# Opening of a three-layer kernel: half-size condition loads, context rows moved behind the first turned products, filler matmuls, context squares added on GpSimd

## The reference, cut to what matters

```python
sh1, sc1, g1, sh2, sc2, g2 = ada_mod(c, ada_w[0], ada_b[0])        # silu(c) @ w + b, w is 1024 x 6144
csh1, csc1, ... = ada_mod(c_ctx, ada_w[0], ada_b[0])               # the same matrix, other condition
xcn = modulate(rms_norm(ctx, norm_mix_g[0]), csh1, csc1)           # the 256 context tokens
xn  = modulate(rms_norm(x, norm_mix_g[0]), sh1, sc1)               # h * (1 + scale) + shift
proj = xn @ w_in                                                   # fourier input, q, k, v
kv_c = xcn @ w_in[:, Q_END:]                                       # k and v of the context
q, k = rope(q), rope(k); y = concat(fourier_mix(f_in), attention(q, k, v, k_c, v_c)) @ w_out
```

## Time and profile before

| | |
|---|---|
| three runs | 1180.71, 1182.01 and 1186.97 us, median 1182.01 |
| profiled execution | 1183.51 us, its span 1181.7 us |
| PE busy | 96% of the span |
| DVE, ACT, POOL busy | 69%, 50%, 7% |
| chain of waits over the whole span | PE 87%, DVE 7%, ACT 4%, DMA 1%, issue 1% |
| HBM read | 222.76 MB, 189 GB/s over the span |

### The profile page before, as it was taken

How to read it: one execution, slowest core, us unless ns; L and a number is a source line. 1 busy time by engine, 2 the same in 40 slices (tenths; PEclk the granted TensorE clock), 3 DMA queues, 4 the chain that set the end, 5 groups by cost and what they waited for, 6 DMA issues and landing times.

```text
span 1181.7 us, 23984 instructions
## 1 busy us (share of the span) xinstructions
PE 1138.0 (96%) x10258; PEld 1077.9 (91%) x10258; DVE 818.8 (69%) x1496; ACT 591.2 (50%) x1085; POOL 82.1 (7%) x101
## 2 busy tenths in 40 slices
PE   8888799999998999999999999999999999999999
PEld 2786799999997999999989988879999999999998
DVE  6776769988886776555765788879554665877443
ACT  2545555444435544554465657653224545665432
POOL 0000010000011000011100111113500001000000
PEclk9899999999999999999998999999999999999999
DMA  9732938888882567540742423222124555855520
GB/s 389 328 143 95 369 154 338 342 341 329 328 344 104 214 229 282 204 158 31 286 150 101 144 72 108 97 83 73 39 73 143 178 185 183 311 188 205 191 82 14
DMA packets 32220, 225.36 MB, mean 191 GB/s; under 512 B 3569, under 2 KB 4721, under 8 KB 5105
## 3 DMA queue, kind: packets, MB, share of 16 engines
q1 hardware_dynamic: 30530, 221.21, 49.9%
q10 hardware_dynamic: 1584, 2.62, 0.7%
HBM read 222.76 MB, written 1.05 MB: 189 GB/s over the span
## 4 chain that ended last, share of the span: by engine, by line
PE 87%; DVE 7%; ACT 4%; DMA 1%; issue 1%; POOL 0%; POOLq 0%; DVEq 0%
PE bank L567 23%; PE bank L569 23%; PE bank L568 23%; PE bank L1060 2%; PE bank L1051 1%; DVE sb_wlo L1913 1%; PE bank L585 1%; DVE sb_ring L1957 1%; PE bank L594 1%; PE bank L1082 1%; DVE sb_tmp L1942 1%; DMA sb_ring<-in_ada 1%; PE bank L1248 1%; ACT sb_whi L1394 1%; PE bank L1266 1%; PE bank L1262 1%
## 5 line engine op out<-in xcount | busy, mean ns | idle before, releaser
L567 PE MATMUL bank<-sb_xh,sb_whi 128*128 128x256 f32 x1480 | 418.5, 283 | 3.0 <-DVE sb_wlo L1913 2.7
L569 PE MATMUL bank<-sb_xh,sb_wlo 128*128 128x256 f32 x1480 | 411.1, 278 | 0.0
L568 PE MATMUL bank<-sb_xl,sb_whi 128*128 128x256 f32 x1480 | 411.0, 278 | 0.0
L1913 DVE TENSOR_TENSOR sb_wlo<-sb_ring,sb_whi 128x1024 fp32r<-128x1024 f32 x199 | 241.7, 1221 | 126.3 <-ACT sb_whi L1394 126.0
L567 PEld LDWEIGHTS bank<-sb_xh,sb_whi 128*128 128x128 f32 x1480 | 279.2, 189 | 10.8 <-issue 7.1
L568 PEld LDWEIGHTS bank<-sb_xl,sb_whi 128*128 128x128 f32 x1480 | 279.0, 189 | 0.1
L569 PEld LDWEIGHTS bank<-sb_xh,sb_wlo 128*128 128x128 f32 x1480 | 278.8, 188 | 0.0
L1394 ACT ACTIVATE sb_whi<-sb_ring 128x1024 fp32r<-128x1024 f32 x199 | 208.7, 1053 | 93.1 <-PE bank L569 79.5
L1913 DVE TENSOR_TENSOR sb_wlo<-sb_more,sb_whi 128x1024 fp32r<-128x1024 f32 x106 | 128.7, 1224 | 66.5 <-ACT sb_whi L1394 66.5
L567 PE MATMUL bank<-sb_hh,sb_whi 128*128 128x256 f32 x608 | 168.5, 277 | 0.0
L569 PE MATMUL bank<-sb_hh,sb_wlo 128*128 128x256 f32 x608 | 167.9, 276 | 0.0
(11 more groups left out here) (389 smaller groups left out, 1846.4 us busy)
## 6 DMA issues: line engine op xcount, KB each, us to landing
sb_more<-in_w SPq DMA_DIRECT2D x34, 1024.0 KB, 5.6
sb_ring<-in_w SPq DMA_DIRECT2D x32, 1024.0 KB, 5.7
sb_ring<-in_adaT SPq DMA_DIRECT2D x24, 1024.0 KB, 7.7
sb_ring<-in_f SPq DMA_DIRECT2D x22, 1024.0 KB, 4.9
sb_more<-in_adaT SPq DMA_DIRECT2D x20, 1024.0 KB, 8.7
sb_ring<-in_gn SPq DMA_DIRECT2D x8, 1024.0 KB, 4.9
sb_ring<-in_gd SPq DMA_DIRECT2D x8, 1024.0 KB, 4.9
sb_ring<-in_up SPq DMA_DIRECT2D x8, 1024.0 KB, 5.4
```

The lines of the kernel that those rows point to most:

```text
L567: te.matmul(out, wh, rh, start=start, stop=False, skip_group_check=skip)
L568: te.matmul(out, wh, rl, start=False, stop=False, skip_group_check=skip)
L569: return te.matmul(out, wl, rh, start=False, stop=stop, skip_group_check=skip)
L1913: ve.tensor_tensor(lo, x, hi.bitcast(F32), ALU.subtract).then_inc(*lo_dve.up(n))
```

## The change

1. The `ada0` chunks become eight of 128 x 1024 in place of four of 128 x 2048, each with a slot of its own; PE waits for each and signals after each.
2. The context rows of the last scale chunk (`adaT0` 7) move on DVE from the opening to behind `turned(0)` and `turned(1)`, with the scaling of the context behind them.
3. PE runs two filler matmuls ahead of the `shift` transposes and three behind them. `idle` multiplies constants into a bank that nobody reads.
4. The squares of the context are added by GpSimd (tiles 0 to 6), and PE sums two tiles in place of eight; this stands behind q3 in place of q2. The columns of the context move behind f0, the spread behind f1, the application to the second turn of the f loop, and on ACT `deviation("ctx")` behind the last q copy.
5. SP's places for x, the context and the tables move, so that they stand between the same bytes as before.

```diff
     for i in range(4):
         add("adaT0", 1, split=False, first=4 + i)
-        add("ada0", 1, split=False, first=i)
+        add("ada0", 2, UNIT, False, first=2 * i)
...
             for i in range(4):
                 F.used(F.raw("adaT0"))
-                c = F.raw("ada0")
-                w = chunk(c)
-                P.wait_ge(*landed(c))
-                P.wait_ge(*act.at("csil"))
                 for k in (2 * i, 2 * i + 1):
+                    c = F.raw("ada0")
+                    w = chunk(c)
+                    P.wait_ge(*landed(c))
+                    P.wait_ge(*act.at("csil"))
                     for e in range(2):
...
+                    end.then_inc(*pe.up(("ada0", k)))
+                    F.used(c)
...
+            idle(2)
             ps = take(RA, "shift", (dve, "shift"))
             P.wait_ge(*act.at("row", 1))
             for j in range(8):
                 end = te.transpose(ps[:, 2 * j:2 * j + 2], fTrow[:, j * 128:(j + 1) * 128], ident[0:2, 0:2])
             end.then_inc(*pe.up("shift"))
+            idle(3)
 
             def context_squares():
                 ps = take(RA, ("ms", "ctx"), (act, ("sd", "ctx")))
-                for k in range(KT):
-                    P.wait_ge(*act.at("sq", "ctx", k))
-                    end = te.matmul(ps[0:1, 0:T], ones[:, 0:1], sq[:, k, :], start=k == 0, stop=k == KT - 1)
-                end.then_inc(*pe.up(("ms", "ctx")))
+                P.wait_ge(*pool.at("sum", "ctx", KT - 2))
+                te.matmul(ps[0:1, 0:T], ones[:, 0:1], sq[:, 0, :], start=True, stop=False)
+                P.wait_ge(*act.at("sq", "ctx", KT - 1))
+                te.matmul(ps[0:1, 0:T], ones[:, 0:1], sq[:, KT - 1, :], start=False, stop=True).then_inc(*pe.up(("ms", "ctx")))
...
                 if n == 2:
                     rotate(0)
                     rotate(1)
+                else:
                     context_squares()
-                else:
-                    context_columns()
                     rotate(2)
...
                 if j == 0:
+                    context_columns()
+                    rotate(3)
+                if j == 1:
                     spread("ctx")
-                    rotate(3)
...
-                if n == 3:
-                    deviation("ctx")
                 turned_raw(n)
+            deviation("ctx")
...
+            def context_rows(i, c):
+                V.wait_ge(*act.at("cB", 3))
+                for u in range(2):
+                    jj = 8 + 2 * i + u
+                    x = chunk(c)[:, u * 1024:(u + 1) * 1024]
+                    ve.tensor_tensor_reduce(out=x, in0=x, in1=cB[:, 1, :], scale=1.0, scalar=C("ab0", jj, jj + 1),
+                                            op0=ALU.mult, op1=ALU.add, accum_out=cmod[:, jj:jj + 1]).then_inc(*dve.up(("ada", 0, jj)))
+                F.used(c)
...
+                if i < 3:
+                    context_rows(i, c)
...
                 if n == 2:
                     turned(0)
                     turned(1)
+                if n == 3:
+                    context_rows(3, c)
+                    V.wait_ge(*dve.at("ada", 0, 15))
+                    scaled(1, C("nm", 0, 8), cmod[:, 8:16])
             turned(2)
-            V.wait_ge(*pe.at("cd"))
-            ve.reciprocal(dev[:, 1, :], ps_of("cd")[:, 0:2]).then_inc(*dve.up(("rs", "ctx")))
             for j in range(4):
                 weights("mixin")
                 if j == 0:
                     turned(3)
+                if j == 1:
+                    V.wait_ge(*pe.at("cd"))
+                    ve.reciprocal(dev[:, 1, :], ps_of("cd")[:, 0:2]).then_inc(*dve.up(("rs", "ctx")))
                     apply("ctx", ctxr, scl[:, 1, :], cmod[:, 0:8], xch, xcl)
...
             gp.memset(one, 1.0).then_inc(*pool.up("one"))
+            sums("ctx")
...
-                if c == 4:
+                if c == 6:
                     sp.dma_start(h[:, :, :], a["xT"]).then_inc(s_x, 16)
-                if c == 10:
+                if c == 14:
```

More of the change, by code:

```diff
@@ L678, in tensor_program @@
                 F.used(F.raw("adaT0"))
-                c = F.raw("ada0")
-                w = chunk(c)
-                P.wait_ge(*landed(c))
-                P.wait_ge(*act.at("csil"))
                 for k in (2 * i, 2 * i + 1):
+                    c = F.raw("ada0")
+                    w = chunk(c)
+                    P.wait_ge(*landed(c))
+                    P.wait_ge(*act.at("csil"))
                     for e in range(2):
-                        o = (k % 2) * 1024 + e * 512
-                        end = te.matmul(ps_of(("row", e))[0:2, :], csil[:, k, :], w[:, o:o + 512], start=k == 0, stop=k == KT - 1)
-                end.then_inc(*pe.up(("ada0", i)))
-                F.used(c)
+                        end = te.matmul(ps_of(("row", e))[0:2, :], csil[:, k, :], w[:, e * 512:(e + 1) * 512], start=k == 0, stop=k == KT - 1)
+                    end.then_inc(*pe.up(("ada0", k)))
+                    F.used(c)
                 if i == 1:
@@ L1450, in scalar_program @@
                 F.used(F.raw("ada0"))
+                F.used(F.raw("ada0"))
                 if i == 1:
@@ L1985, in vector_program @@
                                             op0=ALU.mult, op1=ALU.add, accum_out=mods[:, 0, jj:jj + 1]).then_inc(*dve.up(("adax", jj)))
-                V.wait_ge(*act.at("cB", 3))
-                for u in range(2):
-                    jj = 8 + 2 * i + u
-                    x = chunk(c)[:, u * 1024:(u + 1) * 1024]
-                    ve.tensor_tensor_reduce(out=x, in0=x, in1=cB[:, 1, :], scale=1.0, scalar=C("ab0", jj, jj + 1),
-                                            op0=ALU.mult, op1=ALU.add, accum_out=cmod[:, jj:jj + 1]).then_inc(*dve.up(("ada", 0, jj)))
-                F.used(c)
+                if i < 3:
+                    context_rows(i, c)
+                F.used(F.raw("ada0"))
                 F.used(F.raw("ada0"))
```

9 lines of the change are left out of this document (4 added, 5 removed).

## The result

The changed kernel takes 1195.99 us, the kernel before 1183.16 (medians of 6 runs each, 1193.1 to 1198.8 and 1180.7 to 1187.0): a ratio of 1.0105, 95% interval 1.0079 to 1.0130, so 12.8 us slower. I had forecast 1188 and a range up to 1191.5. The profiled execution of after took 1197.65 us, that of before 1183.51.

A forecast was written before the change was run, and what follows sets the result against it. PE, busy 96% of the span, was taken to bound the kernel; −1.7 opening, −2.7 squares, +9.4 idle, +2.4 clock, −1.6 old wait, +0.4 spread and columns gave +6.2 us at the scores: 1188.2 us, range 1183.5 to 1191.5.

The forecast's parts named there:

- the sum: Total of all gains and losses up to the first attention's scores: +6.2 us, giving 1188.2 us.
- everything downstream just shifts: Behind the first attention's scores: everything moves by the same amount as the scores, forecast 6.2 us later.
- first q copy on ACT: In the opening: ACT is free for this copy at 42.6 us, before 42.75 with a wait until 43.45.
- to `mixin` 3 landed: Load issued after the context rows, done at 52.4 us, and `adaT0` 8; as second load it takes 7.6, landing at 60.5.
- to the spread behind f1: PE goes on at 62.3 us; columns, rotation and f1 take 3.6 plus 2.4 for low clock, ending at 68.3.
- Row products and filler: In the opening: it starts at 34.7 us, fillers keep PE's clock up, q2 starts at 41.7, gain 1.7 us.
- the opening's loads get a gap: Rival, chance 0.14: `mixin` 0 waits for the slot of `adaT0` 6, up to 3.1 us later for all behind: 1191.3.
- The fillers: Five matmuls of 0.45 us in PE's idle time in the opening: free, and they keep the clock up.
- one of my own two signs of being wrong: The signs: ACT's split of `mixin` 3 finds its chunk landed, or the clock is low in the opening.
- The context squares: PE behind q3: two matmuls of 0.45 us replace eight, gaining 2.7 us; GpSimd's adds cost DVE 1.4.
- The load that is late next: `mixin` 3, behind the moved context rows and `adaT0` 8, lands at 60.5 us; PE idles 9.4 us until 62.3.
- The halves behind the opening: Half-size chunks move the first feed-forward weights to slots freed later, by `mixout`; cost put at nothing.

The follow-up runs named there:

- e3: The kernel before with only `ada0` in eight half-size loads: 1186.05 us, ratio 1.0030.
- e2: The kernel before with only the context rows of `adaT0` 7 and the scale row moved behind `turned(1)`: 1191.08 us, ratio 1.0067.
- e6: The changed kernel with `ada0` in four whole-size loads again: 1187.08 us, ratio 1.0038 against the kernel before.
- e5: The kernel before with only the five filler matmuls around the small transposes: 1184.10 us, ratio 1.0009.
- e7: The changed kernel with whole-size `ada0` loads and the context rows of `adaT0` 7 back in the opening: 1180.08 us, ratio 0.9980 against the kernel before.
- e11: The changed kernel measured and profiled once more, unchanged: 1195.14 us, ratio 1.0094 against the kernel before.
- e8: The kernel before with 19 filler matmuls (8.6 us of PE work) right ahead of the first scores: 1190.68 us, ratio 1.0065.
- e9: The changed kernel with ACT's fourth q copy and context deviation ahead of the split of `mixin` 3's first unit: 1192.75 us, ratio 1.0089 against the kernel before.
- e10: The changed kernel with whole-size `ada0`, context rows in the opening, and the context squares summed by PE alone: 1180.55 us, ratio 0.9968 against the kernel before.
- e4: The kernel before with only GpSimd adding the context's squares, PE's two squares in the old place: 1186.68 us, ratio 1.0029.
- e13: The changed kernel with ACT's deviation ahead of `mixin` 3's split and DVE's reciprocal ahead of `mixin` 4's split: 1193.94 us, ratio 1.0088 against the kernel before.
- e14: The changed kernel with only DVE's reciprocal moved ahead of the split of `mixin` 4's first unit: 1191.83 us, ratio 1.0082 against the kernel before.
- e1: The changed kernel with the context rows of `adaT0` 7 and the scale row back in the opening: 1182.52 us, ratio 0.9996 against the kernel before.

## Why the prediction was wrong

The direction and the wait were right, the size was not. The result is 7.8 us above the 1188.2 of the sum: 2.5 us are missing up to the scores (8.7 later than before, and not 6.2), 4.1 behind them, and 1.2 is the median of before itself (1183.16 over six executions, 1182.01 over the first three). So two steps failed: the opening, and "everything downstream just shifts", which cost more: with the scores 8.7 us later and nothing else, the 1183.16 of before would have become 1191.9. The steps up to the scores, beside the first profile of after:

| step | forecast | after |
|---|---|---|
| first q copy on ACT | 42.6 | 46.12 |
| from there to the context rows done | 9.8 | 9.8 |
| to `mixin` 3 landed | 8.1 | 7.3 |
| to PE going on | 1.8 | 1.8 |
| to the spread behind f1 | 6.0 | 6.1 |
| to the scores | 18.0 | 17.8 |
| scores | 86.3 | 88.9 |

- **The step that failed up to the scores is the first one, "Row products and filler".** It let the opening start at 34.7 and q2 at 41.7, on the premise that `mixin` 0 lands at 29.30 as before. It landed at 32.76 (30.8 to 32.8 in the seven profiles with half-size loads, 29.0 to 29.3 in the nine with whole ones). I had this as a rival of 0.14 ("the opening's loads get a gap", up to 3.1 us), as another case beside the forecast. They are not alternatives: the late `mixin` 0 lies ahead of the late `mixin` 3 and adds in full. e3 shows the first alone (+2.9), e2 the second alone (+8.0), and e6 is without the first. Its time, 1187.08, is within a microsecond of my number for the whole, but by luck: its context rows were done at 52.3, as I had them (52.4), while `mixin` 3 went out first and landed at 57.10 (60.5 forecast), and its scores came at 82.24 and not at 86.3.
- **The fillers.** Right where `mixin` 0 is on time (e5, e7: clock 1.00 from 35 to 41, q2 at 41.8). In after, PE's gap was longer by the lateness of `mixin` 0, and the two fillers stood at its start: 3.73 us of idle time followed, and the clock was 0.50: one of my own two signs of being wrong, in this profile, though not in e11 (1.00). The first q copy came 2.7 us later than before, where I had it 0.9 earlier.
- **The context squares.** Two matmuls instead of eight, as put. PE waited 0.72 us for the last add, which I had at nothing. DVE's delay by the adds: 0.54 and 0.44 on the two pairs of `wlo` (2.90 and 2.89 against 2.36 and 2.45), 0.84 on the two `turned`, 1.8 in all, against 1.4.
- **The load that is late next.** SP, ACT and PE went as written, each piece within 0.8 us. In the terms of the sum some of that is luck: PE was idle 7.9 us and not 9.4, because it reached the wait 4.2 us later than forecast and the load landed 2.7 later; and the 6.1 us from there to the spread are 1.8 for the lower clock, where I had 2.4, and a wait of 0.65 for DVE's reciprocal, which I had at nothing.
- **"Everything downstream just shifts".** This step failed too. For a delay made of work it held (e8). In after, 4.1 us more than the 8.7 at the scores are lost by the medians. In the first profile 1.7 us come between 101 and 110, where the window from 100 to 110 has a clock of 0.83, and 1.6 between 380 and 531. Most of the other edited kernels also end 1 to 3 us worse than their scores (e3: +1.0 and +2.9; e5: -1.5 and, by the ratio, +1.1), e11 4.6 us; e8, e9 and e10 do not, by their medians. What the record shows is where this time goes: into PE's low clock. From the scores to the end PE was busy for 1067.0 us in before, 1070.4 and 1071.3 in the two profiles of after (e11 is the second), and 1064.0 in e8, for the same 9876 matmuls; over all sixteen profiles the time behind the scores (1099 to 1107 us) rises with this busy time. And it is not one execution's chance: the mean granted clock of a whole execution is 0.9815 and 0.9812 in the two sets of after, against 0.986 to 0.989 in the four of before and 0.9885 in e8 (a part of that difference lies ahead of the scores). Why the changed kernel gets the lower clock more often behind its scores, no run shows; this part stays open. The single profile of before may also have been late at the scores by up to 1.5 us (e2 and e4, the same up to there, had the clock at 0.72 in the opening and not 0.50, and finished the second rotation 1.4 to 1.5 us sooner).
- **The halves behind the opening.** I had their slots at "nothing" by looking at `mixout` and the first feed-forward weights. The slots that mattered were those of `mixin` 0 and `adaT0` 8: the new count of chunks put `adaT0` 8 in the slot of `adaT0` 7, so it waits for the moved rows and stands first in the idle queue, ahead of `mixin` 3.

## What to carry to other kernels

Two mishaps on one chain are a sum, not two rivals: before giving a rival a chance of its own, ask whether it lies ahead of the forecast's wait, and if so give the sum its own case. When a plan deals slots in turn, changing the number of chunks changes which consumer every later load waits for; list the slot and the releaser of each load near the change, not only of the ones behind it. And a wait behind a late load may not be mended by reordering the engines that consume it: in e9, e13 and e14 it moved to the next instruction that needs the load or stands behind one that does. Mending the release did help (e1, e7).
